# The low halves of the front's weights on GpSimd instead of VectorE

## The chip, the core and the metric

The kernel runs on one core of a Trainium2 chip. In the profile PE is TensorE, ACT is ScalarE, DVE is VectorE, POOL is GpSimd and SP issues most DMAs. The metric is the device time of one launch in microseconds, the median of several runs. One more launch was profiled; all rows below come from it.

## The reference

One layer of a streaming encoder over 320 tokens (256 of a prompt, 64 of a running stream), all in float32. Cut to what matters:

```
proj = rms_norm(x, norm1_g) @ w_in            # 2048 -> q | k | v | u, 1024 columns each
q, k = partial_rope(rms_norm(q)), partial_rope(rms_norm(k))
s = softmax((q . k) * 64 ** -0.5)             # 8 heads, two score maps each, block-causal
o = rms_norm((s[0] - lam * s[1]) @ v)         # differential attention
h[t] = a * h[t-1] + b u[t]                    # complex state space, 64 groups of 64 states
y = gelu(c h + d u); y = y * sigmoid(y @ w_glu + b_glu)
x = x + concat(o, y) @ w_out
q2 = rms_norm(x, norm2_g) @ w_peer_q          # product-key scores, top 16 of 128 x 128 experts
x = x + sum_k softmax(score)_k * gelu(x . peer_u[k]) * peer_v[k]
```

## The kernel before, in words

Each float32 weight is split into a high half (the weight rounded to the matmul's format, float32r) and a low half, the rest. A product is then three matmuls: high by high, high by low, low by high. Weights stream through `ring`, four slots of 1 MB; a block in it holds four pieces of 128x512. For piece `p`, ACT writes the high half into `w_parts[:, p % 4, 0, :]` (line 505) as soon as PE has used piece `p - 4` (semaphore `w_used`); another engine subtracts it from the ring and writes the low half beside it; PE waits for that and multiplies the piece. So ACT and the low half can be at most four pieces ahead of PE.

The front is pieces 0 to 207: `w_in` is 0 to 127 (0 to 31 give `u`, 32 to 127 give q, k and v), `w_glu` 128 to 143, `w_out` 144 to 207. After it come `w_peer_q` and the experts, 256 pieces of which POOL makes the low halves in a loop (line 478) before DVE takes over. In the front DVE makes the low halves (`front_low`, line 867 with output `w_parts`); its loop over `p` does the low half of piece `p` first and then the job that is planned behind piece `p`. Such a plan, written out as numbers at the head of the file and as conditions on `p`, sets the order on PE, ACT and DVE:

- DVE, pieces 0 to 36: low halves of x (`x_low`), powers of the state matrix, input matrices (`weighted_inputs`, eight of them, three products of 128x1024 each), the norm of x, `inputs_out` which writes `u` (the second half of it behind piece 34). PE may go past piece 36 only with all of `u`, since `own_kernels` follows that piece.
- DVE, pieces 72 to 85: the recurrence (`state_step`, `carry`, `carry_inside`, `states_turned`, semaphore `hc`). Behind it DVE and POOL each make half of eight output matrices (`output_powers`: DVE signals `ca`, POOL `cb`), which PE takes from piece 88 on (`group_outputs`).
- pieces 123 to 169: attention, 24 units of one head and one token tile. Unit `u` stands at piece 123 + 3u/2: PE makes scores behind it (line 1644, 1646), DVE the row maximum four pieces on (`score_max`, line 1131), ACT the exponentials, DVE the head weights six pieces on (`head_weights`, lines 1144 to 1146), PE the transposed weights and the values. There is one pair of banks for scores, so the scores of unit `u + 1` wait for the exponentials of unit `u`.

POOL, before, does its own jobs one behind the other, each behind the semaphore that it needs, and no low half in the front.

Of the kernel before, what the change touches and what calls it, by code (L numbers as in the profile page):

```python
# [7 lines left out]
F32 = mybir.dt.float32  # L8
# [4 lines left out]
ALU = mybir.AluOpType  # L13
# [3 lines left out]
P = 128  # L17
# [4 lines left out]
NT = len(TILES)  # L22
# [7 lines left out]
STEP = 8  # L30
# [55 lines left out]
def build(nc, io):  # L86
# [8 lines left out]
    with ctx:  # L95
# [214 lines left out]
        def key_half(n, half):  # L310

            return 128 * n + 64 * (half + 1) if n < 2 else KEYS_OF[2]
# [11 lines left out]
        def ca_cols(ap):  # L324
            return ap.rearrange("p g (j n) -> p g j n", j=STEP)
# [99 lines left out]
        @block.gpsimd  # L425
        def _(pool):
            for dst, src in S5IN:
                pool.dma_start(dst, src).then_inc(S["s5in"], 16)
            pool.memset(ones1, 1.0).then_inc(S["ones"], 1)
            for j in range(4):  # L430
                two = [slice(4 * j + 2 * k, 4 * j + 2 * k + 2) for k in range(2)]
                pool.wait_ge(S[f"x{j}"], 16)
                pool.tensor_tensor(sq1[:, 4 * j:4 * j + 4, :], x_raw[:, 4 * j:4 * j + 4, :], x_raw[:, 4 * j:4 * j + 4, :], ALU.mult).then_inc(S["sq1"], 1)
                pool.wait_ge(S["sq1"], 2 * j + 1)
                pool.tensor_tensor(sq1[:, two[0], :], sq1[:, two[0], :], sq1[:, two[1], :], ALU.add).then_inc(S["sq1"], 1)

            pool.wait_ge(S["wt_tr"], 16)
            pool.memset(Tm, 0.0).then_inc(S["tz"], 1)
            pool.wait_ge(S["tz"], 1)
            pool.wait_ge(S["k7o"], 3)  # L440
            pool.tensor_copy(Tm[:, :, P - SSM_P:], k7.rearrange("p (g n) -> p g n", g=GROUPS)).then_inc(S["tz"], 1)

            pool.wait_ge(S["hp"], 1)
            pool.dma_start(io["states"][:, 0, :], HP[:, SEGS - 2, SEG, :]).then_inc(S["h_out"], 16)
            pool.dma_start(io["states"][:, 1, :], HP[:, SEGS - 1, SEG, :]).then_inc(S["h_out"], 16)
            pool.wait_ge(S["hc"], 1)
            for x in range(8):
                rr, ri, cre, cim, ncim = ca_parts(x)
                if x >= 2:
                    pool.wait_ge(S["y_mm"], x - 1)  # L450
                pool.tensor_tensor(ca_cols(CA[x % 2][1]), rr, ncim, ALU.mult).then_inc(S["cb"], 1)
                pool.tensor_tensor(ca_cols(tmp_ca[1]), ri, cre, ALU.mult).then_inc(S["cb"], 1)
                pool.wait_ge(S["cb"], 3 * x + 2)
                pool.tensor_tensor(CA[x % 2][1], CA[x % 2][1], tmp_ca[1], ALU.subtract).then_inc(S["cb"], 1)
                pool.wait_ge(S["cb"], 3 * x + 3)

            pool.wait_ge(S["ca"], 8)
            pool.wait_ge(S["k_ok"], NT)
            pool.wait_ge(S["y_sv0"], 16 * STEP)
            pool.dma_start(yT[:, 0:4, :], io["y_tmp"].rearrange("(b p) t -> p b t", p=P)[:, 0:4, :]).then_inc(S["y_in0"], 16)  # L460
            pool.wait_ge(S["y_mm"], 8)
            for u in range(3):
                for n in range(2):
                    for c in range(2):
                        a = key_half(n, 0)
                        pool.memset(sm[u][0:64, c, a:a + 64], 0.0).then_inc(S["zeros"], 1)
            pool.wait_ge(S["y_sv1"], 16 * STEP)
            pool.dma_start(yT[:, 4:8, :], io["y_tmp"].rearrange("(b p) t -> p b t", p=P)[:, 4:8, :]).then_inc(S["y_in1"], 16)
            pool.wait_ge(S["o_ok"], NT)
            pool.memset(ones2, 1.0).then_inc(S["ones"], 1)  # L470

            def low_parts(first, end):

                with pool.Fori(0, (end - first) // SLOTS) as i:
                    for k in range(SLOTS):
                        for q in range(4):
                            pool.wait_ge(S["w_hi"], i * (4 * SLOTS) + (4 * (first + k) + q + 1))
                            pool.tensor_tensor(w_parts[:, q, 1, :], ring[:, k, 512 * q:512 * (q + 1)], w_parts[:, q, 0, :].bitcast(F32),  # L478
                                               ALU.subtract).then_inc(S["w_lo"], 1)

            low_parts(B_PQ, B_DVE)

            pool.wait_ge(S["sid"], 64)
            pool.wait_ge(S["gs_mm"], TP // 4)
            for g in range(2 * PICKED):
                b, k = g % 3, g % PICKED
                if g >= 3:
                    pool.wait_ge(S["row_used"], g - 2)
                table = io["peer_u_rows"] if g < PICKED else io["peer_v"].rearrange("k p n -> (k p) n")
                pool.indirect_dma_start(rows[b], None, table, bass.IndirectOffsetOnAxis(ap=ids[:, k:k + 1], axis=0)).then_inc(S[f"gr{b}"], 16)  # L490
# [3 lines left out]
        def _(act):  # L494
# [40 lines left out]
            def kernels_out(i):  # L535
                j, half = divmod(i, 2)
                n = SSM_P * (j + 1)
                act.wait_ge(S["tm_mm"], i + 1)
                act.wait_ge(S["tz"], 1)
                act.activation(Tm[0:n, 32 * half:32 * half + 32, 16 * j:16 * j + 16], psum[0:n, 6 + half, :].rearrange("p (g n) -> p g n", g=GP),  # L540
                               ACT.Copy).then_inc(S["tm"], 1)

# [320 lines left out]
        def _(dve):  # L863
# [6 lines left out]

                return dve.tensor_scalar(dst, src, 1.0 / n, EPS, ALU.mult, ALU.add)

            def front_low(p):
                b, q = divmod(p, 4)
                dve.wait_ge(S["w_hi"], p + 1)
                tt(w_parts[:, q, 1, :], ring[:, b % SLOTS, 512 * q:512 * (q + 1)], w_parts[:, q, 0, :].bitcast(F32),
                   ALU.subtract).then_inc(S["f_lo"], 1)

            def x_low(dc):
                dve.wait_ge(S["x_hi1"], dc + 1)  # L880
                for to, of in ((slice(384, 640), slice(0, TP)), (slice(T, 384), slice(TP, T))):
# [216 lines left out]
            def heads_normed(kind, n):  # L1098
                r = TILES[n][1]
                v = (q_tok, k_tok)[kind][0:r, n, :].rearrange("p (h d) -> p h d", d=HD)  # L1100
                heads = (r, 16, HD)
                dve.wait_ge(S["hstd"], NT * kind + n + 1)
                if kind == n == 0:
                    dve.wait_ge(S["tm_mm"], 14)
                    dve.wait_ge(S["tz"], 2)
                chain(dve.reciprocal(hr[0:r, :], hv[0:r, :]))
                chain(tt(v, v, spread(hr[0:r, :].unsqueeze(2), *heads), ALU.mult))
                chain(tt(v, v, spread(qk_g[0:r, kind, :].unsqueeze(1), *heads), ALU.mult))
                a, b = v[:, :, 0:8], v[:, :, 8:16]
                cosr, sinr = (spread(rope[0:r, n, 8 * i:8 * i + 8].unsqueeze(1), r, 16, 8) for i in range(2))  # L1110
                m = [rt[0:r, k, :].rearrange("p (h d) -> p h d", d=8) for k in range(4)]
                for k, (e, f) in enumerate(((a, cosr), (b, sinr), (b, cosr), (a, sinr))):
                    chain.add(tt(m[k], e, f, ALU.mult))
                chain.wait()
                chain.add(tt(a, m[0], m[1], ALU.subtract))
                chain(tt(b, m[2], m[3], ALU.add))
                dve.sem_inc(S[("q_ok", "k_ok")[kind]], 1)
# [75 lines left out]
            for p in range(4 * B_PQ):  # L1193
# [4 lines left out]
                if p in (139, 147):  # L1198
# [3 lines left out]
                        gated(k0 + k)  # L1202
                        s_low(k0 + k - 1)
                    s_low(k0 + 3)
                front_low(p)
                if p == 2:
                    lambdas()
                if p == 3:
# [272 lines left out]
        def _(pe):  # L1481
# [95 lines left out]
            def group_outputs(g):  # L1577
                x, par, gp = g // 8, g % 2, g // 2
                fill = 2 * (gp // 12) + par
                if g == 0:  # L1580
                    pe.wait_ge(S["tm"], 14)
                    pe.wait_ge(S["tz"], 2)
                    pe.wait_ge(S["fs"], 6)
                    pe.wait_ge(S["hc"], 1)
                if g % 8 == 0:
                    pe.wait_ge(S["ca"], x + 1)
                    pe.wait_ge(S["cb"], 3 * x + 3)
                if gp % 12 == 0 and fill >= 4:
                    pe.wait_ge(S["y_gl"], fill - 3)
                pr = slice(64 * par, 64 * par + 64)  # L1590
                out = psum[:, 4 + fill % 4, CH * (gp % 12):CH * (gp % 12) + CH]
                pe.matmul(out, Tm[:, g, :], UG[:, g, :], start=True, stop=False)  # L1592
                pe.matmul(out, CA[x % 2][0][pr, gp % 4, :], HCt[pr, gp, :], start=False, stop=False)  # L1593
                ins = pe.matmul(out, CA[x % 2][1][pr, gp % 4, :], HCt[pr, GP + gp, :], start=False, stop=True)  # L1594
                if g % 8 == 7:
                    ins.then_inc(S["y_mm"], 1)
# [376 lines left out]
```

## Time and profile before

| | |
|---|---|
| median of 3 runs | 2510.91 us (2505.94 to 2514.09) |
| profiled execution | 2503.37 us, span of its instructions 2501.3 us |
| mean granted clock of PE | 0.957 |
| busy share of the span | PE 92%, PEld (weight loads) 88%, DVE 67%, ACT 44%, POOL 23% |
| busy time, instructions | PE 2295.2 us, 17069; DVE 1681.4 us, 2885; POOL 575.2 us, 447 |

The front takes the first 700 us of the span. In it the busy share of PE swings, and PE's idle time is named by what it waited for. A busy time of PE is modelled and says little on its pace, so steps between pieces are taken from the instructions in order of time.

### The profile page before, as it was taken

To read this page: it belongs to the slowest core of one execution; us is meant where nothing else is said; L and a number is where in the kernel's file an instruction comes from. 1 tells how busy PE (TensorE), PEld (TensorE's weight loads), DVE (VectorE), ACT (ScalarE), POOL (GpSimd) and SP (SyncE) were. 2 spreads that over 40 slices of the span, in tenths; PEclk is the share of its full clock that TensorE was granted. 3 is DMA by queue.
4 is the path that set the end of the run, shared out by engine and by line. 5 is a ranking of instruction groups with operands and counts; after the bars stand their busy time and mean duration, and the time that the engine had idled before them with its cause. 6 is when DMAs were issued, how large, how long until landed. Compare 5 with 4: busy or idle time off the path is not lost.

```text
span 2501.3 us, 43312 instructions
## 1 busy us (share of the span) xinstructions
PE 2295.2 (92%) x17069; PEld 2190.8 (88%) x17069; DVE 1681.4 (67%) x2885; ACT 1098.5 (44%) x2058; POOL 575.2 (23%) x447
## 2 busy tenths in 40 slices
PE   5799999778956998988969999999999999999999
PEld 4786787667956998988869999999999999999998
DVE  6936764565432579177827888877768888877866
ACT  3224224654322453544434444444454444444444
POOL 3001221000022689844731111111101111111100
PEclk9899879789986999999989999999999999999999
DMA  5362115312322344566667888888868888888854
GB/s 186 106 138 85 69 47 164 135 68 68 132 87 101 135 160 137 188 187 192 215 228 297 331 336 342 307 314 312 314 255 310 330 347 330 311 317 319 336 203 159
DMA packets 128077, 537.67 MB, mean 215 GB/s; under 512 B 27648, under 2 KB 63920, under 8 KB 67216
## 3 DMA queue, kind: packets, MB, share of 16 engines
q1 hardware_dynamic: 59584, 358.11, 40.5%
q0 software_dynamic: 19200, 136.70, 13.1%
q10 hardware_dynamic: 49168, 41.21, 5.4%
q8 instruction: 76, 1.25, 0.2%
q14 instruction: 49, 0.40, 0.1%
HBM read 507.02 MB, written 28.38 MB: 214 GB/s over the span
## 4 chain that ended last, share of the span: by engine, by line
PE 58%; issue 22%; POOL 11%; DVE 5%; DMA 1%; ACTq 1%; POOLq 0%; ACT 0%; DVEq 0%
PE psum L1485 16%; PE psum L1486 16%; PE psum L1487 16%; POOL w_parts L478 11%; DVE experts L867 3%; PE psum L1509 2%; PE psum L1511 1%; PE psum L1510 1%; DVE w_parts L867 1%; PE psum L1593 1%; DMA experts<-xs_tmp 1%; PE psum L1592 1%; ACTq L497 1%; PE psum L1514 1%; PE psum L1515 1%
## 5 line engine op out<-in xcount | busy, mean ns | idle before, releaser
L505 ACT ACTIVATE w_parts<-ring 128x512 fp32r<-128x512 f32 x1296 | 817.4, 632 | 1165.2 <-PE psum L1487 958.2
L867 DVE TENSOR_TENSOR w_parts<-ring,w_parts 128x512 fp32r<-128x512 f32 x1040 | 711.2, 695 | 506.7 <-ACT w_parts L505 490.7
L1485 PE MATMUL psum<-x_parts,w_parts 128*128 128x256 f32 (+1 forms) x2624 | 785.6, 299 | 70.8 <-DVE x_parts L867 37.7
L1487 PE MATMUL psum<-x_parts,w_parts 128*128 128x256 f32 (+1 forms) x2624 | 771.9, 294 | 0.0
L1486 PE MATMUL psum<-x_parts,w_parts 128*128 128x256 f32 (+1 forms) x2624 | 771.8, 294 | 0.0
L1485 PE MATMUL psum<-h_parts,w_parts 128*128 128x256 f32 x2048 | 581.3, 284 | 21.2 <-DVE h_parts L867 21.2
L1485 PEld LDWEIGHTS psum<-x_parts,w_parts 128*128 128x128 f32 x2624 | 513.3, 196 | 90.0 <-POOL w_parts L478 65.4
L1486 PE MATMUL psum<-h_parts,w_parts 128*128 128x256 f32 x2048 | 580.8, 284 | 0.0
L1487 PE MATMUL psum<-h_parts,w_parts 128*128 128x256 f32 x2048 | 580.6, 284 | 0.0
L1486 PEld LDWEIGHTS psum<-x_parts,w_parts 128*128 128x128 f32 x2624 | 514.6, 196 | 0.7
L1487 PEld LDWEIGHTS psum<-x_parts,w_parts 128*128 128x128 f32 x2624 | 514.1, 196 | 0.0
L478 POOL TENSOR_TENSOR w_parts<-ring,w_parts 128x512 fp32r<-128x512 f32 x256 | 358.4, 1412 | 297.7 <-ACT w_parts L505 289.3
L1485 PEld LDWEIGHTS psum<-h_parts,w_parts 128*128 128x128 f32 x2048 | 394.5, 193 | 21.8 <-DVE h_parts L867 10.8
L1486 PEld LDWEIGHTS psum<-h_parts,w_parts 128*128 128x128 f32 x2048 | 394.6, 193 | 0.0
L1487 PEld LDWEIGHTS psum<-h_parts,w_parts 128*128 128x128 f32 x2048 | 394.4, 193 | 0.0
L867 DVE TENSOR_TENSOR experts<-experts 128x256 f32<-128x256 f32 (+9 forms) x329 | 195.6, 605 | 64.2 <-PE psum L1594 31.9
L490 POOL DMA_INDIRECT experts<-in_peer_v,experts x64 | 73.8, 1153 | 480.2 <-DVE experts L1423 393.2
L490 POOL DMA_INDIRECT experts<-in_peer_u_rows,experts x64 | 73.3, 1145 | 464.0 <-DVE experts L1418 458.1
L1423 DVE SCALAR_TENSOR_TENSOR experts<-experts 128x2048 f32<-128x2048 f32 x63 | 147.7, 2345 | 0.0
L1418 DVE SCALAR_TENSOR_TENSOR experts<-experts 128x2048 f32<-128x2048 f32 x64 | 146.3, 2285 | 0.0
L867 DVE TENSOR_TENSOR experts<-psum,experts 128x1024 f32<-128x1024 f32 (+4 forms) x138 | 112.9, 854 | 12.3 <-PE psum L1487 11.9
L1509 PE MATMUL psum<-w_parts,x_parts 128*128 128x512 f32 x192 | 89.9, 468 | 10.0 <-DVE w_parts L867 9.3
(215 smaller groups left out, 1997.7 us busy)
## 6 DMA issues: line engine op xcount, KB each, us to landing
ring<-in_peer_u SPq DMA_DIRECT2D x128, 1024.0 KB, 4.9
ring<-in_peer_v SPq DMA_DIRECT2D x128, 1024.0 KB, 4.8
ring<-in_w_in SPq DMA_DIRECT2D x32, 1024.0 KB, 4.8
ring<-in_w_out SPq DMA_DIRECT2D x16, 1024.0 KB, 4.9
ring<-in_w_pq SPq DMA_DIRECT2D x16, 1024.0 KB, 4.8
g_tmp<-experts ACTq DMA_DIRECT2D x16, 1024.0 KB, 8.0
experts<-g_tmp ACTq DMA_DIRECT2D x16, 1024.0 KB, 7.1
experts<-in_xT SPq DMA_DIRECT2D x8, 640.0 KB, 9.3
```

The lines of the kernel that those rows point to most:

```text
L478: pool.tensor_tensor(w_parts[:, q, 1, :], ring[:, k, 512 * q:512 * (q + 1)], w_parts[:, q, 0, :].bitcast(F32), ALU.subtract).then_inc(S["w ...
L490: pool.indirect_dma_start(rows[b], None, table, bass.IndirectOffsetOnAxis(ap=ids[:, k:k + 1], axis=0)).then_inc(S[f"gr{b}"], 16)
L497: act.dma_start(dst, src).then_inc(S["consts"], 16)
L505: act.activation(w_parts[:, q, 0, :], ring[:, b % SLOTS, 512 * q:512 * (q + 1)], ACT.Copy).then_inc(S["w_hi"], 1)
L867: return dve.tensor_tensor(out, a, b, op)
L1418: dve.scalar_tensor_tensor(row, row, 1.0, xs, ALU.mult, ALU.mult, accum_out=dots[:, k:k + 1]).then_inc(S["row_used"], 1)
L1423: dve.scalar_tensor_tensor(accs, row, coef[:, k:k + 1], accs, ALU.mult, ALU.add).then_inc(S["row_used"], 1)
L1485: pe.matmul(out, w_parts[:, q, 0, c], moving(0), start=start, stop=False)
L1486: pe.matmul(out, w_parts[:, q, 0, c], moving(1), start=False, stop=False)
L1487: return pe.matmul(out, w_parts[:, q, 1, c], moving(0), start=False, stop=stop)
L1509: pe.matmul(o, xh, w_parts[:, q, 0, :], start=dc == 0, stop=False)
L1510: pe.matmul(o, xh, w_parts[:, q, 1, :], start=False, stop=False)
```

## The change

`front_low` moves from DVE's program to POOL's, with the same operands and the same semaphore (`f_lo`), so that PE, ACT and SP see no other condition. POOL's own jobs are divided and put behind given pieces in one loop over `p`: the clearing of `Tm` and its copy in four parts (pieces 69 to 72; the last 16 columns are no longer cleared first), the saving of the states behind piece 82, `output_powers` in its three operations behind pieces 86 to 110, the two loads of y and the zeros behind pieces 113 to 121, the ones behind 182. Waits for `tz` count eight parts. DVE loses its 208 low halves and nothing else.

```diff
+            def front_low(p):
+                b, q = divmod(p, 4)
+                pool.wait_ge(S["w_hi"], p + 1)
+                pool.tensor_tensor(w_parts[:, q, 1, :], ring[:, b % SLOTS, 512 * q:512 * (q + 1)], w_parts[:, q, 0, :].bitcast(F32),
+                                   ALU.subtract).then_inc(S["f_lo"], 1)
+            def output_powers(x, part):
...
+                if part == 0:
+                    if x >= 2:
+                        pool.wait_ge(S["y_mm"], x - 1)
+                    pool.tensor_tensor(ca_cols(CA[x % 2][1]), rr, ncim, ALU.mult).then_inc(S["cb"], 1)
+                elif part == 1:
+                    pool.tensor_tensor(ca_cols(tmp_ca[1]), ri, cre, ALU.mult).then_inc(S["cb"], 1)
+                else:
+                    pool.wait_ge(S["cb"], 3 * x + 2)
+                    pool.tensor_tensor(CA[x % 2][1], CA[x % 2][1], tmp_ca[1], ALU.subtract).then_inc(S["cb"], 1)
+                    pool.wait_ge(S["cb"], 3 * x + 3)
+            for p in range(4 * B_PQ):
+                front_low(p)
+                if 69 <= p < 73:
+                    g = 16 * (p - 69)
+                    if p == 69:
+                        pool.wait_ge(S["wt_tr"], 16)
+                        pool.wait_ge(S["k7o"], 3)
+                    pool.memset(Tm[:, g:g + 16, 0:P - SSM_P], 0.0).then_inc(S["tz"], 1)
+                    pool.tensor_copy(Tm[:, g:g + 16, P - SSM_P:], k7.rearrange("p (g n) -> p g n", g=GROUPS)[:, g:g + 16]).then_inc(S["tz"], 1)
+                if p == 82:
+                    pool.wait_ge(S["hp"], 1)
...
+                if p == 86:
+                    pool.wait_ge(S["hc"], 1)
+                for x in range(8):
+                    for part in range(3):
+                        if p == (86 + 2 * x + part // 2 if x < 2 else 87 + 3 * x + part):
+                            output_powers(x, part)
+                if p == 113:
+                    pool.wait_ge(S["ca"], 8)
+                    pool.wait_ge(S["k_ok"], NT)
+                    pool.wait_ge(S["y_sv0"], 16 * STEP)
...
@@ the vector engine
-            def front_low(p):
-                b, q = divmod(p, 4)
-                dve.wait_ge(S["w_hi"], p + 1)
-                tt(w_parts[:, q, 1, :], ring[:, b % SLOTS, 512 * q:512 * (q + 1)], w_parts[:, q, 0, :].bitcast(F32),
-                   ALU.subtract).then_inc(S["f_lo"], 1)
...
-                front_low(p)
                 if p == 2:
                     lambdas()
```

DVE's order in the attention, before, around pieces 141 and 142 (L867 on `w_parts` is a low half, L1144 to L1146 are the head weights of units 8 and 9, L1131 and L1134 the maximum of unit 10):

```order
L867 TENSOR_TENSOR w_parts<-ring,w_parts 128x512
L1144 RECIPROCAL small<-small 128x2
L1145 SCALAR_TENSOR_TENSOR small<-small 128x1
L1146 SCALAR_TENSOR_TENSOR experts<-experts,small 128x256
L867 TENSOR_TENSOR w_parts<-ring,w_parts 128x512
L1144 RECIPROCAL small<-small 128x2
L1145 SCALAR_TENSOR_TENSOR small<-small 128x1
L1146 SCALAR_TENSOR_TENSOR experts<-experts,small 128x256
L1131 TENSOR_REDUCE small<-psum 64x2 x2
L1134 TENSOR_SCALAR small<-small 128x2
```

The same place of DVE's program now (L1161 to L1163 are the head weights, L1148 and L1151 the maximum):

```order
L1161 RECIPROCAL small<-small 128x2
L1162 SCALAR_TENSOR_TENSOR small<-small 128x1
L1163 SCALAR_TENSOR_TENSOR experts<-experts,small 128x256
L1161 RECIPROCAL small<-small 128x2
L1162 SCALAR_TENSOR_TENSOR small<-small 128x1
L1163 SCALAR_TENSOR_TENSOR experts<-experts,small 128x256
L1148 TENSOR_REDUCE small<-psum 64x2 x2
L1151 TENSOR_SCALAR small<-small 128x2
```

The two low halves, and with them the waits for ACT's high halves, are gone from between the three jobs.

POOL's order behind the recurrence, before (the saving of the states, then the first of the output matrices):

```order
L444 DMA out_states<-experts 128x64
L445 DMA out_states<-experts 128x64
L451 TENSOR_TENSOR experts<-experts 128x512
L452 TENSOR_TENSOR experts<-experts 128x512
L454 TENSOR_TENSOR experts<-experts 128x512
```

The same place now (L440 is a low half; pieces 83 to 86 stand together, then 87 and 88):

```order
L468 DMA out_states<-experts 128x64
L469 DMA out_states<-experts 128x64
L440 TENSOR_TENSOR w_parts<-ring,w_parts 128x512 x4
L449 TENSOR_TENSOR experts<-experts 128x512
L451 TENSOR_TENSOR experts<-experts 128x512
L440 TENSOR_TENSOR w_parts<-ring,w_parts 128x512
L454 TENSOR_TENSOR experts<-experts 128x512
L440 TENSOR_TENSOR w_parts<-ring,w_parts 128x512
```

The low halves of pieces 87 and 88 now stand behind POOL's wait for `hc` and behind two or three of its products.

## Rows read from the trace of the kernel before

**Rows 1.** Busy time by stretch: window, us, PE, PEld, DVE, ACT, POOL, granted clock, DMA.

```profile
22.00:129.00 107.00, 82.12 (x453) 76.00 (x454) 101.89 (x239) 35.31 (x63) 4.25 (x2) 0.94 0.33 111
...
270.00:412.00 142.00, 139.64 (x627) 117.64 (x628) 83.92 (x119) 33.06 (x53) 33.92 (x34) 0.80 0.24 73
412.00:616.00 204.00, 160.28 (x911) 135.54 (x910) 115.55 (x252) 114.91 (x325) 0.97 (x2) 0.86 0.30 108
616.00:700.00 84.00, 80.51 (x519) 76.59 (x517) 33.27 (x57) 30.79 (x55) 1.29 (x1) 0.98 0.35 126
```

**Rows 2.** What PE waited for, 20 to 129 us: sum in us, times, longest.

```profile
PE psum L1492 <- DVE w_parts L867: 41.4, 10, 25.5
PE psum L1509 <- DVE w_parts L867: 5.5, 3, 2.6
```

**Rows 3.** What PE waited for, 425 to 616 us.

```profile
PE psum L1644 <- ACT experts L596: 26.4, 8, 6.7
PE psum L1646 <- ACT experts L596: 6.9, 4, 3.6
...
PE psum L1485 <- DVE experts L867: 3.8, 1, 3.8
```

**Rows 4.** Instructions in order of time, DVE: start, us, line and operation, [idle before].

```profile
56.62 3.59 DVE L867 TENSOR_TENSOR experts<-experts 128x512 f32<-128x512 f32 x5
...
104.93 1.29 DVE L867 TENSOR_TENSOR w_parts<-ring,w_parts 128x512 fp32r<-128x512 f32 x2
106.14 3.61 DVE L867 TENSOR_TENSOR experts<-experts 128x1024 f32<-128x1024 f32 x3
...
120.39 0.28 DVE L867 TENSOR_TENSOR experts<-experts 128x64 f32<-128x64 f32 x1
```

**Rows 5.** DVE alone by stretch: busy us, granted clock, DMA.

```profile
22.00:121.00 99.00, 94.57 (x212) 0.93 0.29 103
222.00:264.20 42.20, 39.44 (x90) 1.00 0.25 90
```

**Rows 6.** DVE, instructions that write or read psum alone, the first of these stretches.

```profile
22.00:121.00 99.00, 8.04 (x26) 0.93 0.29 103
```

**Rows 7.** DVE, groups by form, 22 to 121 us: busy us, mean ns.

```profile
L993 DVE RECIPROCAL experts<-experts 128x320 f32<-128x320 f32 x1 | 2.1, 2141 | 0.0
```

**Rows 8.** Both engines at work: DVE in order of time.

```profile
264.76 4.80 DVE L867 TENSOR_TENSOR experts<-experts 128x512 f32<-128x512 f32 x3
...
942.94 3.27 DVE L867 TENSOR_TENSOR experts<-experts 128x2048 f32<-128x2048 f32 x1
```

**Rows 9.** POOL in order of time: an output matrix's first product, and a low half.

```profile
264.32 1.48 POOL L451 TENSOR_TENSOR experts<-experts 128x512 f32<-128x512 f32 x1 [12.54 <-DVE experts L1078]
...
757.72 1.26 POOL L478 TENSOR_TENSOR w_parts<-ring,w_parts 128x512 fp32r<-128x512 f32 x1 [4.84 <-ACT w_parts L505]
```

**Rows 10.** PE in order of time, around pieces 37, 87 and 88.

```profile
125.61 0.39 PE L1539 MATMUL psum<-experts 128*128 128x32 f32 x2
128.57 0.50 PE L1509 MATMUL psum<-w_parts,x_parts 128*128 128x512 f32 x1 [2.58 <-DVE w_parts L867]
...
271.12 0.80 PE L1509 MATMUL psum<-w_parts,x_parts 128*128 128x512 f32 x1 [2.58 <-DVE w_parts L867]
...
275.77 0.50 PE L1509 MATMUL psum<-w_parts,x_parts 128*128 128x512 f32 x1 [1.23 <-DVE w_parts L867]
```

**Rows 11.** PE in order of time: scores of unit 10, then of unit 11.

```profile
494.03 0.70 PE L1644 MATMUL psum<-experts 64*128 64x256 f32 x4
...
499.66 1.23 PE L1644 MATMUL psum<-experts 64*128 64x256 f32 x4 [2.53 <-ACT experts L596]
```

**Rows 12.** DVE in order of time between these scores.

```profile
494.58 0.69 DVE L867 TENSOR_TENSOR w_parts<-ring,w_parts 128x512 fp32r<-128x512 f32 x1 [0.69 <-ACT w_parts L505]
...
496.15 1.28 DVE L1131 TENSOR_REDUCE small<-psum 64x2 f32<-64x384 f32 x2
```

**Rows 13.** Busy time by stretch, one stretch of the attention, columns as in the first group.

```profile
444.70:454.80 10.10, 8.38 (x31) 7.54 (x31) 3.97 (x10) 6.43 (x21) 0.00 (x0) 0.50 0.40 126
```

More of the change, by code:

```diff
@@ L435, in _ @@
                 pool.tensor_tensor(sq1[:, two[0], :], sq1[:, two[0], :], sq1[:, two[1], :], ALU.add).then_inc(S["sq1"], 1)
[L437 to L444, printed above, removed]
@@ L445, in _ @@
-            pool.dma_start(io["states"][:, 1, :], HP[:, SEGS - 1, SEG, :]).then_inc(S["h_out"], 16)
-            pool.wait_ge(S["hc"], 1)
-            for x in range(8):
-                rr, ri, cre, cim, ncim = ca_parts(x)
[L449 to L470, printed above, removed]
+            def front_low(p):
[3 more added lines that the diff above has]
+                                   ALU.subtract).then_inc(S["f_lo"], 1)
@@ new lines, in _ @@
+            for p in range(4 * B_PQ):
[9 more added lines that the diff above has]
+                    pool.wait_ge(S["hp"], 1)
+                    pool.dma_start(io["states"][:, 0, :], HP[:, SEGS - 2, SEG, :]).then_inc(S["h_out"], 16)
+                    pool.dma_start(io["states"][:, 1, :], HP[:, SEGS - 1, SEG, :]).then_inc(S["h_out"], 16)
+                if p == 86:
[8 more added lines that the diff above has]
+                    pool.wait_ge(S["y_sv0"], 16 * STEP)
+                    pool.dma_start(yT[:, 0:4, :], io["y_tmp"].rearrange("(b p) t -> p b t", p=P)[:, 0:4, :]).then_inc(S["y_in0"], 16)
+                if 114 <= p < 117:
+                    if p == 114:
+                        pool.wait_ge(S["y_mm"], 8)
+                    for n in range(2):
+                        for c in range(2):
+                            a = key_half(n, 0)
+                            pool.memset(sm[p - 114][0:64, c, a:a + 64], 0.0).then_inc(S["zeros"], 1)
+                if p == 121:
+                    pool.wait_ge(S["y_sv1"], 16 * STEP)
+                    pool.dma_start(yT[:, 4:8, :], io["y_tmp"].rearrange("(b p) t -> p b t", p=P)[:, 4:8, :]).then_inc(S["y_in1"], 16)
+                if p == 182:
+                    pool.wait_ge(S["o_ok"], NT)
+                    pool.memset(ones2, 1.0).then_inc(S["ones"], 1)
@@ L538, in kernels_out @@
                 act.wait_ge(S["tm_mm"], i + 1)
-                act.wait_ge(S["tz"], 1)
+                act.wait_ge(S["tz"], 8)
                 act.activation(Tm[0:n, 32 * half:32 * half + 32, 16 * j:16 * j + 16], psum[0:n, 6 + half, :].rearrange("p (g n) -> p g n", g=GP),
@@ L1104, in heads_normed @@
                     dve.wait_ge(S["tm_mm"], 14)
-                    dve.wait_ge(S["tz"], 2)
+                    dve.wait_ge(S["tz"], 8)
                 chain(dve.reciprocal(hr[0:r, :], hv[0:r, :]))
@@ L1581, in group_outputs @@
                     pe.wait_ge(S["tm"], 14)
-                    pe.wait_ge(S["tz"], 2)
+                    pe.wait_ge(S["tz"], 8)
                     pe.wait_ge(S["fs"], 6)
```

## The prediction

> **What bounds the front now.** I read the busy time by stretch first, then PE's waits, then DVE, POOL and PE in order of time. The front has three places where PE stands still. From 22 to 129 us DVE is busy 101.89 of 107 us and PE only 82.12 [rows 1]; PE waits there for low halves, 41.4 and 5.5 us [rows 2]. This is a stretch bound by DVE: its low halves come late because its state-space jobs stand between them. From 129 to about 268 us PE sets the pace. Around 271 and 276 us PE waits twice more for a low half, 2.58 and 1.23 us, which stand behind the end of the recurrence [rows 10]. From 270 to 412 us PE has hardly an idle microsecond, at a granted clock of 0.80 [rows 1]. From 412 to 616 us PE is busy 160.28 of 204 us; it waits 26.4 and 6.9 us in twelve waits for ACT's exponentials, and once 3.8 us for DVE [rows 3]. Past 616 us low halves hide.
>
> **What a low half costs on either engine.** On DVE two of them take 1.21 us from start to start, 104.93 to 106.14 [rows 4]: 0.60 us each. On POOL one takes 1.26 us [rows 9]; beside PE's three pieces of lead that latency hides. The question is what POOL's does to DVE while it runs. Undisturbed, DVE's product of 128x512 takes 3.59 / 5 = 0.72 us and that of 128x1024 3.61 / 3 = 1.20 us [rows 4]; by that slope (0.48 us for 512 elements) one of 128x2048 takes 2.17. Beside POOL's low halves it took 3.27 us, 1.1 us more; beside POOL's own products of 128x512 the 128x512 took 4.80 / 3 = 1.60 us, 0.88 more [rows 8]. So the two engines do not share, they take turns, and each low half on POOL that meets a DVE operation with two operands in SBUF stops DVE for 0.88 to 1.1 us; I take 1.0, the middle of two close ends. That is more than the 0.60 us that DVE saves. Operations on psum and the reciprocal I take as free of this.
>
> The Trainium skill says the same as a rule (page "SBUF — State Buffer", section "Who interferes with whom"): a DVE instruction with two SBUF inputs contends with a GpSimd instruction that reads SBUF, and the loser blocks fully. The trace agrees, with the 1.1 us above. It speaks against this change wherever DVE is the bound; by it alone the first term below would be a loss, and a gain has to come from where DVE merely stood in line.
>
> **Pieces 0 to 36.** The end of this stretch is DVE's `inputs_out` at 120.39 + 0.28 us [rows 4]; the four small products of `own_kernels` behind piece 36 need it and take about 0.9 us up to 126.0, and piece 37 starts at 128.57 since its low half waits for one more DVE job [rows 10]. DVE runs from 22.5 to 120.7: 98.2 us, of which 35 low halves are 35 x 0.60 = 21.0. The rest, 77.2 us, stays. Into it POOL now puts low halves 0 to 40, as PE stops behind piece 36 and POOL may be four ahead: 41. Of the 77.2 us, 8.04 are on psum and 2.1 a reciprocal [rows 6, 7], so 87% are blocked when a low half comes: 41 x 0.87 x 1.0 = 35.7 us. The end moves to 22.5 + 77.2 + 35.7 = 135.4, piece 37 to 136.3: **7.7 us later**. The 2.58 us behind `segment_powers` are already in this, since that wait goes. Bounds: with no blocking, 100.6 us and a gain of 28; with all 41 at 1.1 us, 22.5 + 77.2 + 45.1 + 0.9 = 145.7, a loss of 17. The rows on taking turns leave little room for the first.
>
> **Recurrence and output matrices.** From 222 to 264.2 us DVE is busy 39.44 of 42.2 us [rows 5]; 14 low halves of 0.60 leave it (8.4), 14 on POOL block it (14.0): `hc` comes at 269.8 instead of 264.2. POOL is woken by it (before at 264.32 [rows 9]), does two products in turns with DVE's (3.2 us), then low half 87 (1.26): piece 87 at 274.3 instead of 271.12. Then one product and low half 88: 1.6 + 1.26 later, 277.1, against 275.77 for piece 88 before [rows 10]. Low halves 87 and 88 are queued behind POOL's wait for `hc`, but before they were queued behind the same work on DVE. **1.4 us later**; bounds: 6 earlier without blocking, 5 later if POOL's products wait for each of DVE's. From there to piece 111 PE is the bound and POOL's one product per piece fits; the pieces that PE takes straight behind their low half lose the 0.57 us by which POOL is slower: **0.6 us**. The clearing of `Tm` in four parts between low halves 69 to 73 uses up most of the lead there; I cost it at nothing, and at 2 us if DVE's first steps block POOL's copies.
>
> **Attention.** In units of even number the maximum starts late. Unit 10: its scores run from 494.03 for 0.70 us, so they are there at 494.73, but the maximum starts at 496.15 [rows 11, 12]. Before it DVE ran head weights of unit 8, then waited 0.69 us for ACT's high half of piece 142 and made its low half (494.58), then head weights of unit 9 [rows 12]. Without the low halves both head weights run as soon as their exponentials are there, before the scores end, and the maximum starts right behind the scores: 496.15 - 494.73, less about 0.1 for the start, is 1.3 us earlier, and so are the exponentials and the scores of unit 11, which waited 2.53 us [rows 11]. Read in this way, and limited by the wait itself, the twelve waits give 1.2, 3.3, 1.2, 2.2, 0.6, 1.3, 2.4, 1.3, 0.9, 0.6, 1.9 and 1.3 us: 18 of the 33.3. Two (units 8 and 14) are long because of the gating of y and keep most of their length. The wait of 3.8 us is behind the output norm, which stood behind two low halves: 1.5 us. From this I take off 4.5 us for low halves that block head weights and output norms: **15 us earlier**, bounds 6 (if ACT or PE is late next) and 19.5.
>
> **The clock.** After such an idle stretch PE ran at a clock of 0.50, 1.2 GHz, for instance 10.1 us from 444.7 [rows 13], behind one of the twelve waits, while from 616 to 700 us, with hardly an idle place, it had 0.98 [rows 1]. Where four of the waits shrink to about a microsecond, up to four such stretches may go, at most 40 us at half the pace, 20 us of time. They are not all that long, and PE does not bound all of them: I take **6 us earlier**, bounds 0 and 20.
>
> **Sum.** 7.7 + 1.4 + 0.6 - 15 - 6 = -11.3 us against the profiled execution's 2503.37 us: 2492. The median of the runs is 7.5 us above that execution, so on its scale the forecast is 2500 us, its own range 2485 to 2512. This measurement tells a difference from no change from about 0.3%, 7.5 us, on.
>
> **Rivals.**
> - *Blocking takes more than the queue gives.* One mechanism, at one place: in pieces 0 to 36 every low half stops DVE, also by way of copies and short chained operations that lose their turn each time. Then 17 us are lost there, 3 in the recurrence, and the attention gives 10 without help of the clock: +11, 2522 us. It decides from about 0.9 us of DVE time per low half on all 41. For it: DVE is busy 94.57 of 99 us there [rows 5]. Against it: on psum and reciprocals nothing is lost. Chance 0.20.
> - *The attention's waits are bound anew.* The maximum is earlier, but ACT, which serves exponentials, high halves and copies in one order, or PE's pieces, are late next: 6 to 7 us gained there, no clock, 9.7 lost before: +3, 2513 us. For it: ACT is busy 114.91 of 204 us [rows 1]; against it: for all twelve waits the exponentials are named, and nothing else [rows 3]. Chance 0.25.
> - *DVE and POOL do not stop each other there* (low halves slip into DVE's pauses): 28 and 6 us gained, then the attention as above: about 2445 us. Against it are the rows above. Chance 0.05.
>
> The forecast has 0.50. **Chances:** faster by over 0.3% is 0.45 of the forecast's 0.50, the third rival's 0.05, 0.03 of the second: 0.53. Within 0.3%: 0.05 of the forecast, 0.18 of the second, 0.03 of the first: 0.26. Slower: 0.21. The range that holds the time 8 times in 10 runs from 2476 (bounds of attention and clock together) to 2521.
>
> **What would show it.** Piece 37 should start at about 136 us; at 128 or before, blocking is smaller than I take it, past 140 larger. DVE's 128x1024 products in that stretch should take 2.2 us where a low half meets them. `hc` should come about 47 us behind the last state input instead of 42. The maxima of most even units should start right behind their scores, and PE's twelve waits should sum to about 15 us. If past piece 208 anything but the start has moved, or a low half makes PE wait in the attention, the account is wrong.

## The result, and the profile after

The changed kernel took 2518.8 us (median of 20 runs) against 2505.9 us of the kernel before (20 runs on the same chip): the ratio is 1.0055, with a 95% interval of 1.0033 to 1.0077. Measured once more beside the experiments it was 1.0035 (1.0012 to 1.0057). The change made the kernel slower, by 9 to 14 us. 2500 us and "faster" were forecast; the time lies inside the range, the direction is wrong. One launch among the experiments, in e1, took 7248 us at a granted clock of 0.31 and is in no ratio.

The profiled execution took 2525.84 us, its span is 2524.0 us and the mean granted clock 0.948; this one lies 7 us above the median of its runs. DVE is busy for 1634.6 us (1681.4 before), POOL for 870.3 us (575.2). The stretches that answer to [rows 1], moved by about what the start of their pieces had moved (columns as there):

```profile
25.00:138.00 113.00, 79.69 (x452) 75.64 (x452) 107.41 (x185) 32.58 (x58) 70.56 (x42) 0.86 0.26 93
...
290.00:440.00 150.00, 149.07 (x622) 125.49 (x623) 84.68 (x89) 32.76 (x52) 81.92 (x65) 0.73 0.22 68
440.00:640.00 200.00, 156.04 (x918) 131.96 (x917) 96.18 (x197) 115.75 (x326) 74.29 (x56) 0.88 0.33 116
640.00:724.00 84.00, 79.64 (x516) 75.77 (x514) 9.61 (x23) 31.50 (x58) 47.95 (x38) 0.99 0.33 113
```

In the first of them DVE has 39 low halves less to make (28 us of the row before) and is yet busy for 107.41 us instead of 101.89. In the attention (third row) it has 19 us less to do, and yet pieces 117 to 172, which hold the attention, are only 7 us shorter.

What PE waited for in the first stretch (sum, times, longest) shows another picture than [rows 2]. The first line is the start of the kernel; 25.5 of the 41.4 us in [rows 2] are that too, so low halves behind the start cost PE 21.4 us before.

```profile
PE psum L1508 <- POOL w_parts L440: 28.1, 1, 28.1
PE psum L1554 <- DVE experts L890: 23.0, 1, 23.0
PE psum L1508 <- DVE x_parts L899: 7.3, 4, 4.2
```

Apart from that first wait, low halves make PE wait nowhere here now. PE runs ahead, reaches piece 36 at 111.3 us (123.2 before), and then stands for 23.0 us before `own_kernels` (L1554), which need DVE's last job. The low halves' waits were turned into one wait for the rest of DVE's work.

Where the time went is told by the start of each piece's first product on PE, in order of time, changed kernel minus kernel before. Beside the profiled run stand two further executions of the changed kernel, e8 and e10 below:

| stretch | forecast | profiled run | e8 | e10 |
|---|---|---|---|---|
| up to piece 37 | +7.7 | +9.4 | +7.9 | +9.7 |
| pieces 37 to 86 (all of it in 37 and 38) | 0 | +4.0 | +2.1 | +4.2 |
| pieces 86 to 88, the recurrence's end | +1.4 | +5.3 | +5.3 | +5.3 |
| pieces 88 to 117 | +0.6 | +11.3 | +0.3 | +10.9 |
| pieces 117 to 172, attention and clock | -21 | -6.9 | -8.5 | -8.9 |
| pieces 172 to 207 | 0 | 0.0 | 0.0 | 0.0 |
| sum | -11.3 | +23.1 | +7.1 | +21.2 |

**The turns.** DVE, then POOL, in order of time (start, us, engine, line, operation, how many):

```profile
103.19 6.56 DVE L890 TENSOR_TENSOR experts<-experts 128x1024 f32<-128x1024 f32 x3
...
120.44 10.92 DVE L890 TENSOR_TENSOR experts<-experts 128x1024 f32<-128x1024 f32 x9
...
135.89 0.28 DVE L890 TENSOR_TENSOR experts<-experts 128x64 f32<-128x64 f32 x1
```

```profile
104.17 14.01 POOL L440 TENSOR_TENSOR w_parts<-ring,w_parts 128x512 fp32r<-128x512 f32 x7
```

Three products of 128x1024 beside low halves take 6.56 / 3 = 2.19 us each, nine of them, when POOL has stopped, 10.92 / 9 = 1.21 us: 0.98 us for each meeting. POOL's low half is stretched too, to 14.01 / 7 = 2.0 us against 1.26 alone [rows 9]. The last job of the stretch, which ended at 120.67 us before [rows 4], now ends at 136.17. Against the 99.7 us at which 22.5 + 77.2 us of work alone would have ended, 36.5 us are lost to 41 low halves, 0.89 us each.

**The recurrence's end.** DVE's two products of the carry at 270 us, and POOL in order of time:

```profile
270.45 6.07 DVE L890 TENSOR_TENSOR experts<-experts 128x224 f32<-128x224 f32 x2
```

```profile
270.69 0.54 POOL L469 DMA_DIRECT2D out_states<-experts  x1
271.25 5.01 POOL L440 TENSOR_TENSOR w_parts<-ring,w_parts 128x512 fp32r<-128x512 f32 x4
286.09 1.61 POOL L449 TENSOR_TENSOR experts<-experts 128x512 f32<-128x512 f32 x1 [9.83 <-DVE experts L1095]
287.66 1.55 POOL L451 TENSOR_TENSOR experts<-experts 128x512 f32<-128x512 f32 x1
289.17 1.70 POOL L440 TENSOR_TENSOR w_parts<-ring,w_parts 128x512 fp32r<-128x512 f32 x1
```

Low halves 83 to 86 had piled up behind POOL's wait for `hp`; they run in one burst of 5.01 us, and the two small products take 6.07 us (a pair of this form takes 0.68 us undisturbed, at 278.41). `hc` comes 49.6 us behind the last state input (286.01, the end of DVE's copy L1095, less 236.39) instead of 41.3; low half 87 is done 4.86 us later, and PE waits 8.94 us for it:

```profile
290.93 0.80 PE L1525 MATMUL psum<-w_parts,x_parts 128*128 128x512 f32 x1 [8.94 <-POOL w_parts L440]
```

**The attention.** PE's waits there, to set against [rows 3]:

```profile
PE psum L1660 <- ACT experts L619: 24.9, 9, 6.7
PE psum L1501 <- ACT experts L658: 5.8, 4, 3.6
PE psum L1501 <- DVE experts L890: 4.8, 1, 4.8
PE psum L1662 <- ACT experts L619: 4.5, 3, 2.5
```

24.9 + 4.5 = 29.4 us for the exponentials, again in twelve waits, instead of 33.3; the wait behind the output norm grew from 3.8 to 4.8 us, and that for other work of ACT (L658 here, L635 before) from 4.0 to 5.8. Once PE waits for a low half, 1.3 us at piece 117, ahead of the first scores. So PE as a whole hardly stands still for less time. This is PE alone in pieces 117 to 172, before and then now (window, us, busy us, granted clock, DMA):

```profile
413.00:623.00 210.00, 166.37 (x943) 0.85 0.30 109
```

```profile
443.00:646.00 203.00, 160.32 (x943) 0.88 0.32 113
```

It is idle for 43.6 us before and for 42.7 now (42.5 in e8, 44.1 in e10). What makes the stretch shorter is the pace of the same 943 products, at a higher granted clock.

At the place of [rows 11, 12], unit 10, ACT and then DVE in order of time:

```profile
519.78 0.63 ACT L528 ACTIVATE w_parts<-ring 128x512 fp32r<-128x512 f32 x1 [1.78 <-PE psum L1503]
520.32 0.35 ACT L638 ACTIVATE experts<-psum,small 128x128 f32<-128x128 f32 x1
```

```profile
520.70 0.17 DVE L1161 RECIPROCAL small<-small 128x2 f32<-128x2 f32 x1 [4.79 <-ACT experts L638]
520.90 0.89 DVE L1162 SCALAR_TENSOR_TENSOR small<-small 128x1 f32<-128x1 f32 x1
521.83 0.48 DVE L1163 SCALAR_TENSOR_TENSOR experts<-experts,small 128x256 f32<-128x256 f32 x1
522.35 1.27 DVE L1148 TENSOR_REDUCE small<-psum 64x2 f32<-64x384 f32 x2
```

The scores of this unit ended at 520.60, and the maximum still starts 1.75 us later; 0.67 us of that is L1162, which takes 0.89 us beside a low half and 0.22 without one (e4). DVE stands idle for 4.79 us in front of the head weights of unit 9. It waits for L638, which is `values_out` of unit 6: `head_weights(u)` may write `rz` only when ACT has read the `rz` of three units before. On ACT that job stands behind the high half L528, which waits for PE. The low half went, and DVE stands in the same queue by another wait.

### The profile page after: what moved, and what is told of

It is laid out like the page before. It is cut to its first block, busy times and chain, and to the rows that moved or that the text cites. A ratio compares the mean times of both kernels' runs of the same rounds, so it can differ in the third digit from the quotient of the medians.

```text
span 2524.0 us, 43303 instructions
## 1 busy us (share of the span) xinstructions
PE 2303.6 (91%) x17069; PEld 2199.3 (87%) x17069; DVE 1634.6 (65%) x2677; ACT 1098.6 (44%) x2058; POOL 870.3 (34%) x661
## 4 chain that ended last, share of the span: by engine, by line
PE 62%; issue 14%; POOL 11%; DVE 9%; ACT 2%; ACTq 1%; DMA 1%; POOLq 0%; DVEq 0%
PE psum L1501 17%; PE psum L1503 17%; PE psum L1502 17%; POOL w_parts L501 11%; DVE experts L890 5%; PE psum L1525 2%; PE psum L1527 1%; PE psum L1526 1%; PE psum L1609 1%; DMA experts<-xs_tmp 1%; DVE x_parts L899 1%; PE psum L1608 1%; PE psum L1530 1%; PE psum L1531 1%; ACT experts L619 1%
## 5 line engine op out<-in xcount | busy, mean ns | idle before, releaser
L528 ACT ACTIVATE w_parts<-ring 128x512 fp32r<-128x512 f32 x1296 | 817.4, 632 | 1173.0 <-PE psum L1503 964.7
L890 DVE TENSOR_TENSOR w_parts<-ring,w_parts 128x512 fp32r<-128x512 f32 x832 | 562.7, 689 | 307.0 <-ACT w_parts L528 296.4
L501 POOL TENSOR_TENSOR w_parts<-ring,w_parts 128x512 fp32r<-128x512 f32 x256 | 358.6, 1412 | 219.8 <-ACT w_parts L528 211.5
L440 POOL TENSOR_TENSOR w_parts<-ring,w_parts 128x512 fp32r<-128x512 f32 x208 | 295.8, 1431 | 289.3 <-ACT w_parts L528 288.8
L890 DVE TENSOR_TENSOR experts<-experts 128x256 f32<-128x256 f32 (+9 forms) x329 | 231.4, 714 | 78.1 <-PE psum L1610 32.5
```

The lines of the kernel that those rows point to most:

```text
L440: pool.tensor_tensor(w_parts[:, q, 1, :], ring[:, b % SLOTS, 512 * q:512 * (q + 1)], w_parts[:, q, 0, :].bitcast(F32), ALU.subtract).then_ ...
L528: act.activation(w_parts[:, q, 0, :], ring[:, b % SLOTS, 512 * q:512 * (q + 1)], ACT.Copy).then_inc(S["w_hi"], 1)
L890: return dve.tensor_tensor(out, a, b, op)
```

## The experiments

Ratios are to the kernel before on the same chip, with a 95% interval. e5 has 6 runs, e10 and e11 are one execution each, the others have 12 runs.

**e1: the first 41 low halves back on DVE.**

```diff
             for p in range(4 * B_PQ):
-                front_low(p)
+                if p == 41:
+                    pool.wait_ge(S["f_lo"], 41)
+                if p >= 41:
+                    front_low(p)
@@ the vector engine: front_low as before
+                if p < 41:
+                    front_low(p)
```

> VectorE makes low halves 0 to 40 as before, GpSimd 41 to 207 and its own jobs as in the changed kernel. Theory 1 (the loss is made in pieces 0 to 36: there GpSimd's low halves stop VectorE, whose last job ends at 136.2 us instead of 120.7, and the half clock behind the 23.0 us in which TensorE stands still makes 13.4 us of it): piece 37 starts at about 128.6 again, and the time falls by some 13 us, from 2519 to about 2506, level with the kernel before. Rival (the lasting loss comes later, from the clock between 290 and 440 us, 0.73 instead of 0.80, some 10 us, or from the recurrence): piece 37 is early again, but the time falls by less than 6, to 2513 or more.

Ratio 0.9999 (0.9979 to 1.0019), so some 9 to 14 us below the changed kernel. Piece 37 starts at 128.0 us (128.6 before). This is theory 1's forecast. Its remark on the clock does not hold: pieces 37 and 38 took 4.3 us longer than before in this execution although PE had waited only 2.6 us there, so a half clock at this place does not need the long wait (in e2, behind the same wait, they took as long as before). Pieces 86 to 88 are 5.3 us late as in the changed kernel. The profiled execution, 2519.6 us, lies 8 us above the median; its pieces 88 to 117 took 146.2 us.

**e2: low halves 0 to 123 on DVE, POOL only beside attention.** The edit is that of e1 with 124 for 41.

> VectorE makes low halves 0 to 123, so all of the state space's, GpSimd only 124 to 207, those beside attention. Theory 1 (state space loses about 20 us, attention wins about 7): 2506 - 7 = 2499 us, faster than the kernel before, its 12 waits for exponentials some 7 us shorter. Rival (what attention seemed to win is only time that a front that comes late gets back by itself): 2506 or more, the waits as before.

Ratio 0.9979 (0.9952 to 1.0005), median 2500.6 us. By the runs alone this is not told from no change. In the trace pieces 117 to 172 take 201.8 us instead of 210.3, while everything up to piece 88 stands as before (pieces 88 to 117 took 132.3 us instead of 137.1): the 7 to 9 us of the attention are real and not a late front catching up. The theory had the waits for exponentials 7 us shorter; they sum to 30.1 us, 3 us less, and all idle time of PE there is 42.2 us, 1.4 less. The rest lies in PE's pace, at a granted clock of 0.89 instead of 0.85.

**e3: half a low half.** In pieces 0 to 40 POOL subtracts 256 of the 512 columns; the others are left out (a clearing at the start, not shown here, makes them zero).

```diff
+                n = 256 if p < 41 else 512
-                pool.tensor_tensor(w_parts[:, q, 1, :], ring[:, b % SLOTS, 512 * q:512 * (q + 1)], w_parts[:, q, 0, :].bitcast(F32),
+                pool.tensor_tensor(w_parts[:, q, 1, 0:n], ring[:, b % SLOTS, 512 * q:512 * q + n], w_parts[:, q, 0, 0:n].bitcast(F32),
```

> The changed kernel, but GpSimd makes only 256 of the 512 columns of low halves 0 to 40 (the other columns of the low halves are left out, they are zero there). Theory 1 (VectorE is stopped for as long as GpSimd's instruction runs): half the length takes back half of 41 x 0.87 x 1.0 = 36 us, so VectorE's last job ends at 118 to 120 us instead of 136.2, piece 37 starts at 120 to 123 us, and the time is some 16 us less, 2503. Rival (each meeting costs VectorE a fixed time, whatever the length): the end stays at 133 to 136 us and the time at 2516 to 2519.

Ratio 0.9957 (0.9932 to 0.9981). The end of the same job on DVE, and then piece 37 on PE:

```profile
117.83 0.28 DVE L893 TENSOR_TENSOR experts<-experts 128x64 f32<-128x64 f32 x1
```

```profile
119.89 0.77 PE L1528 MATMUL psum<-w_parts,x_parts 128*128 128x512 f32 x1
```

The job ends at 118.1 instead of 136.2 us: of the 36.5 us lost, 18.1 are back, half for half the length. What DVE loses goes with the length of POOL's instruction; a fixed price for a meeting is out. The median was 2503.8 us, 2503 had been forecast.

**e4: a fourth buffer for `rz` in the changed kernel.**

```diff
-        mx, nb, z, rz = stat(3, 2), stat(3, 2), stat(3, 2), stat(3, 2)
+        mx, nb, z, rz = stat(3, 2), stat(3, 2), stat(3, 2), stat(4, 2)
...
-                if u >= 3:
-                    dve.wait_ge(S["o_out"], u - 2)
+                if u >= 4:
+                    dve.wait_ge(S["o_out"], u - 3)
```

(and `u % 4` where `rz` is written and read)

> The changed kernel with four buffers for rz instead of three, so that head weights of a unit need not wait until ScalarE has read rz of the unit three before it (values_out). Theory 2 (in the changed kernel the row maxima of the even units stand behind head weights that wait for values_out, which is queued on ScalarE behind a high half; this took the place of the wait for low halves): the maxima of units 4, 6, 10, 12, 16, 18, 20 and 22 start within 0.1 to 0.5 us of their scores instead of 1 to 3.5, the waits for exponentials sum to about 17 us instead of 29.4, and the time falls by 8 to 12, to 2507 to 2511. Rival (ScalarE's own order or TensorE's pieces are next in line): less than 3 us, 2516 or more.

Ratio 0.9990 (0.9960 to 1.0019). DVE at unit 10 in order of time; its scores ran from 497.49 to 498.20:

```profile
495.25 0.17 DVE L1161 RECIPROCAL small<-small 128x2 f32<-128x2 f32 x1 [1.23 <-ACT experts L619]
495.45 0.22 DVE L1162 SCALAR_TENSOR_TENSOR small<-small 128x1 f32<-128x1 f32 x1
495.70 0.49 DVE L1163 SCALAR_TENSOR_TENSOR experts<-experts,small 128x256 f32<-128x256 f32 x1
498.24 1.28 DVE L1148 TENSOR_REDUCE small<-psum 64x2 f32<-64x384 f32 x2 [2.06 <-PE psum L1660]
```

Now the head weights wait for their exponentials (L619) and are done 2 us ahead of the scores; the maximum starts 0.04 us behind these. This holds for units 4, 6, 10, 16 and 18 within 0.4 us, not for 12, 20 and 22 (2.3, 0.75 and 3.5 us). PE's waits for exponentials sum to 20.5 + 2.5 = 23.0 us, more than the 17 expected, and pieces 117 to 172 take 193.4 us, 10 less than in the changed kernel; PE's idle time there falls from 42.7 to 34.9 us. Theory 2 holds for the wait that it names; in the three other units something else is late, which was not followed up.

**e5: e2 and e4 together.**

> Low halves 0 to 123 on VectorE, 124 to 207 on GpSimd (as e2_dve_0_123), and four buffers for rz (as e4_rz_4). Theories 1 and 2 together: the gains add up, since they lie in different waits: some 8 us below e2's, 15 to 20 us below the kernel before, 2490 to 2495 us; pieces 117 to 172 take about 193 us. Rival (each alone takes the same wait away, or the next engine binds): no more than e2, 2500 us.

Median 2488.6 us, ratio 0.9908 (0.9884 to 0.9931): faster than both kernels. The gains add up; pieces 117 to 172 take 192.6 us, 9.2 less than in e2, where 8 had been expected. By the runs e5 lies some 23 us below the kernel before, where 15 to 20 had been forecast; what the rest is, is not shown. The waits for exponentials:

```profile
PE psum L1671 <- ACT experts L622: 20.3, 9, 6.6
...
PE psum L1673 <- ACT experts L622: 2.5, 1, 2.5
```

**e6: no burst.** POOL's wait for `hp` and the two DMA issues stand behind low half 86.

```diff
-                if p == 82:
+                if p == 86:
                     pool.wait_ge(S["hp"], 1)
```

> The changed kernel with GpSimd's wait for hp and its two DMA issues behind low half 86 instead of 82, so that low halves 83 to 86 are no longer made in one burst when hp comes. Theory 3 (the burst of four low halves stops one small VectorE product of the carry for 5.8 us instead of 0.4, on the way to hc): no VectorE product of more than 2.5 us there, hc 2 to 5 us earlier against piece 86, and piece 87 late by 2 to 4 us instead of 6.35. Rival (four low halves stop VectorE for 4 to 5 us in any order): piece 87 late by 5 us or more.

Ratio 1.0003 (0.9981 to 1.0026). No product takes 5.8 us any more. The pair that took 6.07 us, and POOL's low halves 83 to 86:

```profile
269.83 1.78 DVE L890 TENSOR_TENSOR experts<-experts 128x224 f32<-128x224 f32 x2
```

```profile
263.80 2.59 POOL L440 TENSOR_TENSOR w_parts<-ring,w_parts 128x512 fp32r<-128x512 f32 x2 [3.42 <-ACT w_parts L528]
267.19 1.29 POOL L440 TENSOR_TENSOR w_parts<-ring,w_parts 128x512 fp32r<-128x512 f32 x1 [0.81 <-ACT w_parts L528]
269.89 1.48 POOL L440 TENSOR_TENSOR w_parts<-ring,w_parts 128x512 fp32r<-128x512 f32 x1 [1.41 <-ACT w_parts L528]
```

But three other products of DVE, 0.18 to 0.23 us long alone, now take 1.19, 1.29 and 1.29 us, and piece 87 is 5.3 us late against piece 86 instead of 6.35. My theory 3 falls: the rival's "four low halves cost 4 to 5 us in any order" is what happened. `hc` comes 1.1 us earlier against piece 86, not 2 to 5. The lower time of this execution lies in other places: pieces 88 to 117 took 132.2 us. The interval of the ratio meets that of the changed kernel's second measurement.

**e7: the fourth buffer in the kernel before.** The edit is that of e4.

> The kernel before with four buffers for rz. Theory 2 (in the kernel before the head weights stand behind VectorE's low halves, which end only 0.4 us behind values_out, so that taking the one wait away alone gives little): pieces 117 to 172 take 207 to 210 us instead of 210.3, the time falls by 0 to 3 us, ratio 0.999 to 1.000. Rival (the wait for values_out alone was the bound from the start, and low halves on VectorE cost attention nothing): 200 to 202 us there, the time 8 to 10 us lower, ratio 0.996 to 0.997.

Ratio 0.9991 (0.9968 to 1.0015); pieces 117 to 172 take 210.2 us, and the waits are those of [rows 3] to 0.1 us:

```profile
PE psum L1644 <- ACT experts L596: 26.5, 8, 6.7
PE psum L1646 <- ACT experts L596: 7.0, 4, 3.6
```

Each of the two waits hides the other: without low halves on DVE and with the fourth buffer the stretch is 17 us shorter, with the buffer alone 0.1, without the low halves alone 7 to 9. These are not waits alone: PE's idle time there is 43.6 us before, 43.9 with the buffer alone, 42.5 to 44.1 in the changed kernel and 34.9 with both; the rest of the 17 us is PE's pace.

**e8, e10 and e11: the changed kernel twice more and the kernel before once more, without an edit; e9: low halves 0 to 87 on DVE** (the edit of e1 with 88 for 41).

> The changed kernel itself once more, beside the others. Theory 1 (the loss up to piece 87 and the gain in attention are fixed by the order of the instructions; what pieces 88 to 117 take varies with the granted clock from run to run): piece 37 at 137 to 138.5 us, piece 87 some 6.4 us later than 86's lag, pieces 117 to 172 in 201 to 204 us again, but pieces 88 to 117 may take anything from 132 to 149 us. Rival (the change itself costs some 10 us in pieces 88 to 117): 146 to 149 us there again. Ratio 1.004 to 1.007 in both.

> VectorE makes low halves 0 to 87, GpSimd 88 to 207: the loss in pieces 0 to 87 is gone, the output matrices and attention are as in the changed kernel. Theory 4 (what pieces 88 to 117 take varies with the granted clock, with or without GpSimd's low halves there): as e2_dve_0_123, ratio 0.995 to 0.999, and pieces 88 to 117 anywhere from 131 to 149 us. Rival (GpSimd's low halves cost some 10 us in pieces 88 to 117, by way of VectorE or of the clock): 143 us or more there and a ratio of 0.999 to 1.002.

> The changed kernel, one more look at pieces 88 to 117 (148 and 137 us in two looks so far). Theory 4: anywhere from 131 to 149 us. Rival: 143 us or more.

> The kernel before, one more look at pieces 88 to 117 (137 us in its first look and with the fourth buffer). Theory 4: anywhere from 131 to 149 us, not 137 again for a reason of its own. Rival: 137 us or less, always below the changed kernel.

Pieces 88 to 117 took 137.4, 148.0 and 134.1 us in e8, e10 and e11, and 151.0 us in e9. One row of busy time for each, first e8, then e10, e11 and e9 (columns as in the stretches above; the last column but two is the granted clock):

```profile
291.00:428.00 137.00, 135.60 (x625) 114.71 (x624) 80.73 (x87) 33.98 (x55) 78.60 (x63) 0.81 0.24 70
```

```profile
295.00:443.00 148.00, 147.13 (x626) 123.88 (x625) 80.19 (x87) 34.81 (x56) 78.71 (x64) 0.74 0.22 65
```

```profile
276.00:410.00 134.00, 134.00 (x625) 113.27 (x626) 78.79 (x116) 34.30 (x55) 30.29 (x31) 0.82 0.24 70
```

```profile
273.00:424.00 151.00, 150.08 (x625) 126.30 (x623) 79.27 (x87) 34.56 (x56) 78.82 (x64) 0.72 0.23 67
```

PE has the same 625 products in all four and hardly waits; what differs is the share of them at 1.2 GHz. The same program is at 137 and at 148 us. So theory 4 is right that no fixed cost stands there, though the 151.0 us of e9 lie above its own range. The loss ahead of piece 88 is gone in e9, as forecast, and in the other stretches e8 came within 1 us of what had been expected of it (table above). It is not shown that POOL's low halves are without influence: of eight profiled executions with them five took 146 to 151 us and three 132 to 137, of five without them all took 132 to 137. The timed runs do not decide it: e9 is at 0.9967 (0.9942 to 0.9993), e2, which has DVE's low halves there, at 0.9979. This stays open.

## Why the prediction was wrong

*What a low half costs on either engine: right.* I took 0.87 x 1.0 us for each of 41; the trace has 0.89. e3 shows that the price goes with the length of POOL's instruction.

*Pieces 0 to 36: right, and short by the clock.* DVE's end was forecast at 135.4 us and came at 136.2, piece 37 at 136.3, and it came at 136.4 to 138.3. e1 takes this loss back. Not in the sum was that PE ran at half pace in pieces 37 and 38: 2 to 4 us in the three executions.

*Recurrence and output matrices: right in kind, the size wrong.* +1.4 were forecast, +5.3 measured. `hc` was to come 47 us behind the last state input and came at 49.6; low half 87 was to follow by 4.5 us and did by 4.9. That a low half stops DVE for about 1 us held here too, but I counted 14 of them. Between the last state input and `hc` there are 15, and POOL's clearing of `Tm` stopped DVE's first steps as well, which I had named (2 us at most) and left out: one copy of 128x64 took 2.09 us (1.19 before). By e6 the order of the last four is worth 1.1 us.

*Attention: this is the step that failed.* "Without the low halves both head weights run as soon as their exponentials are there" is false in the changed kernel: they wait for `values_out`. The profile of before could have told it. The row of [rows 12] names a wait for the high half, and the low half behind it runs until 495.27; ACT's `values_out` (L615 there) ended at 494.80:

```profile
494.45 0.35 ACT L615 ACTIVATE experts<-psum,small 128x128 f32<-128x128 f32 x1
```

The second wait ended 0.47 us ahead of the first and could be seen in no view as a wait. The twelve waits shrank by 3.9 us and not by 18, other waits took most of that back, and PE's idle time in the stretch went from 43.6 to 42.7 us: of the 15 us of this term next to nothing came. With the fourth buffer (e4) the twelve waits shrink by 10.3. The rival "the attention's waits are bound anew" is what happened, and it named ACT's one order of work. That its 6 to 7 us came close to the 7 to 9 is luck: it had them from the waits, with no help of the clock. Its total of +3 was too low since it took my sums for the two stretches ahead.

*The clock: the size by luck.* In the attention the granted clock rose from 0.85 to 0.88 and 0.91, which is all of the gain there that PE's idle time does not explain, some 6 to 9 us. I had priced it at 6 us on top of 15, but from waits that would shrink, and they did not. All ten profiled executions with low halves of these pieces on POOL have 0.88 to 0.91, the three without 0.85 or 0.86; why is not shown.

*The end: right.* Past piece 172 nothing moved in the front.

In sum: +10 to +14 instead of +7.7 up to piece 86, +5.3 instead of +1.4 to piece 88, -7 to -9 instead of -21 in attention. That is +6 to +12, in line with a measured 9 to 14, without pieces 88 to 117, which stay open. Between forecast and measurement lie 20 to 25 us; the attention makes 12 to 14 of them, the recurrence 4, pieces 37 and 38 two to four, the first stretch up to 2. The choice between forecast and rival hung on the attention alone, and the 15 us there were taken from what stood ahead of the maximum in DVE's order, not from every semaphore that each job in between waits for.

Two numbers of the prediction do not follow from its own terms: the third rival's 28, 6 and 21 us give about 2456 on the scale of the runs and not 2445, and the bounds of attention and clock together (19.5 and 20 instead of 15 and 6) give 2481 and not 2476. Neither bears on what failed.

## What to carry to other kernels

Before a wait is counted as a gain, list every wait of the instruction that moves up, those too that are already over in the trace, and read from the other engines when they ended; what lies between the latest and the second latest end is all that the change can give. Where two engines take turns at SBUF, ask what the moved instruction will meet on the other engine: in this kernel a low half on POOL cost DVE 0.89 us beside the state space, for the 0.60 us that DVE was spared, while in the attention, where DVE is busy for 96.2 of 200 us, the stretch became 7 to 9 us shorter, all of it in PE's pace. A spare buffer was worth 0.1 us alone, a shorter queue 7 to 9, and the two together 17, so try them together.

## What the hardware showed beyond this

- A product of DVE can lose its turn several times. In the burst at 271 us one product waited through four low halves (6.07 us for the pair); the same happened in e1 (6.09 us) and in e8 (6.08 us). Between 93 and 118 us, in the same kernel, the two engines alternated strictly. What decides it was not tried.
- A clearing on POOL does not stop DVE's products. Two products of 128x320 beside a POOL MEMSET took 0.51 us each; beside a low half one of 128x160 took 1.42. The copy of 128x64 did have to wait: it ended at 238.78, with the MEMSET that follows the low half (238.73). In the kernel before it ended at 224.44, also with a MEMSET of POOL (224.39). DVE, then POOL, in order of time:

```profile
236.70 2.09 DVE L1069 COPY experts<-small 128x64 f32<-128x64 f32 x1
...
241.03 1.02 DVE L890 TENSOR_TENSOR experts<-experts 128x320 f32<-128x320 f32 x2
```

```profile
237.15 1.58 POOL L464 MEMSET experts<- 128x1792 f32 x1
...
240.52 1.59 POOL L464 MEMSET experts<- 128x1792 f32 x1
```

The Trainium skill (page "SBUF — State Buffer", section "Who interferes with whom") has both: a DVE instruction with two SBUF inputs meets GpSimd's reads and not its writes, and a copy may take the shared pair whole. The trace agrees, with these numbers.
